# Indexer of the sparse attention: rectify on ScalarE, weight and sum the heads on the matrix unit

## The reference, cut to what matters

```python
def block(xs):                       # one block of 128 queries; two blocks in all
    qb, qib, wb, pb, start = xs
    dots = jnp.einsum('bqhd,bsd->bqhs', qib, k_idx)            # 16 index heads of 64
    I = jnp.einsum('bqh,bqhs->bqs', wb, jax.nn.relu(dots))     # weight and sum the heads
    I = jnp.where(causal[None], I, -jnp.inf)
    _, sel = lax.top_k(I, top_k)                               # 64 keys for each query
    ...                                                        # attention over these keys
```

## Time and profile before

| | us |
|---|---|
| median of three timed runs | 2379.22 |
| lowest and highest of them | 2372.86, 2379.34 |
| the profiled execution | 2371.06 |
| its span | 2369.3 |
| PE, DVE busy | 2004.3 (85%), 1880.9 (79%) |
| ACT, POOL busy | 1173.7 (50%), 312.3 (13%) |

### The profile page before, as it was taken

One profiled execution on the slowest core, in us unless ns is written; L12 is line 12 of the kernel. 1 busy time (PEld: TensorE's weight loads), 2 busy tenths in 40 slices (PEclk: granted clock), 3 DMA queues, 4 the chain that ended last, 5 costly groups with the idle time before them and its releaser, 6 DMA issues. The chain is left out here.

```text
span 2369.3 us, 33971 instructions
## 1 busy us (share of the span) xinstructions
PE 2004.3 (85%) x13220; PEld 1835.7 (77%) x13220; DVE 1880.9 (79%) x2572; ACT 1173.7 (50%) x1609; POOL 312.3 (13%) x214
## 2 busy tenths in 40 slices
PE   5998897898887888889877768699878979987898
PEld 4887797898876878877777756599768868877786
DVE  6877867858876988888889876668988765898886
ACT  5555444335445644444444445544455574445554
POOL 0001321320110013210001000031121100321110
PEclk9998998999999989899988889789999988998999
DMA  6774454559987656679877776566777757575786
GB/s 210 258 231 128 150 178 144 186 175 322 307 297 258 206 188 208 194 240 331 306 245 246 256 248 232 185 197 196 233 230 259 262 163 240 165 255 192 255 265 223
DMA packets 295341, 536.89 MB, mean 227 GB/s; under 512 B 31880, under 2 KB 40973, under 8 KB 294157
## 3 DMA queue, kind: packets, MB, share of 16 engines
q1 hardware_dynamic: 294893, 532.62, 69.4%
q10 hardware_dynamic: 288, 2.10, 0.2%
HBM read 532.55 MB, written 2.10 MB: 226 GB/s over the span
## 5 line engine op out<-in xcount | busy, mean ns | idle before, releaser
L1630 DVE SCALAR_TENSOR_TENSOR ring_r<-ring,w 128x1024 fp32r<-128x1024 f32 x807 | 999.0, 1256 | 389.7 <-ACT w L1235 384.5
L143 PE MATMUL ps<-hh_r,w 128*128 128x256 f32 x4160 | 1106.0, 303 | 150.1 <-DVE ring_r L1630 134.4
L1235 ACT ACTIVATE w<-ring 128x1024 fp32r<-128x1024 f32 x807 | 833.6, 1053 | 756.9 <-DMA ring<-in_w_in 324.1
L143 PE MATMUL ps<-hlo,ring_r 128*128 128x256 f32 x4160 | 1078.2, 296 | 0.0
L143 PEld LDWEIGHTS ps<-hh_r,w 128*128 128x128 f32 x4160 | 857.3, 206 | 178.5 <-DVE ring_r L1630 155.3
L143 PEld LDWEIGHTS ps<-hlo,ring_r 128*128 128x128 f32 x4160 | 856.7, 206 | 1.5 <-issue 1.2
L143 PE MATMUL ps<-w,AR_r 128*128 128x512 f32 x736 | 302.9, 412 | 31.0 <-DVE ring_r L1630 30.9
L1630 DVE SCALAR_TENSOR_TENSOR macc<-ring,sm,macc 128x512 f32<-128x512 f32 x360 | 304.3, 845 | 8.1 <-DMA ring<-in_w_mod 1.2
L143 PE MATMUL ps<-ring_r,AR_r 128*128 128x512 f32 x736 | 295.8, 402 | 0.0
L143 PEld LDWEIGHTS ps<-w,AR_r 128*128 128x128 f32 x736 | 143.0, 194 | 78.3 <-DVE ring_r L1630 48.9
L143 PE MATMUL ps<-AR 128*128 128x64 f32 (+5 forms) x1312 | 179.0, 298 | 17.8 <-DVE AR L1626 14.4
(11 more groups left out here) (176 smaller groups left out, 1556.7 us busy)
## 6 DMA issues: line engine op xcount, KB each, us to landing
ring<-in_w_in SPq DMA_DIRECT2D x408, 512.0 KB, 4.6
ring<-in_w_mod SPq DMA_DIRECT2D x192, 512.0 KB, 6.1
ring<-in_w_up SPq DMA_DIRECT2D x176, 512.0 KB, 4.7
ring<-in_w_out SPq DMA_DIRECT2D x96, 512.0 KB, 5.7
ring<-in_w_down SPq DMA_DIRECT2D x88, 512.0 KB, 5.8
ring<-in_w_branch_b SPq DMA_DIRECT2D x16, 512.0 KB, 5.5
ring<-in_w_branch_a SPq DMA_DIRECT2D x16, 512.0 KB, 5.8
X<-in_x SPq DMA_DIRECT2D x2, 1024.0 KB, 5.6
```

The source lines that it names most:

```text
L143: return e.matmul(o, l, x, start=start, stop=stop, skip_group_check=True)
L1235: return e.activation(o, i, ACT.Copy, scale=scale)
L1630: return e.scalar_tensor_tensor(o, a, s, b, op0, op1)
```

## The change

ACT rectifies the scores out of PSUM (two instructions for each head) into `IX0` and `IX1`, and makes four 128 x 128 diagonals `IWD` for each segment, the identity scaled by the two heads' weights for the two query blocks. PE multiplies diagonal and rectified scores and sums all heads in one PSUM bank (g, held from segment 0 to segment 8), always one segment behind the scores. DVE adds the masks straight from that bank in segment 8. POOL and DVE have no more work in segments 0 to 7.

```diff
@@ -183,9 +183,8 @@
     "upv": ["+s", "+z -s@up_dve.conv", "", "-z@up_dve.lo"],
     "bias": ["", *[s for i in range(12) for s in ("", "", f"+b -b@bias_act.e{i}")]],
     "scalex": [],
-    "indexer": ["+a +b -a@idx_dve.a0 -b@idx_dve.b0",
-                *[f"+a +b +s +z -s@idx_pool.g0{i} -z@idx_pool.g1{i} -a@idx_dve.a{i} -b@idx_dve.b{i}"
-                  for i in range(1, 8)]],
+    "indexer": ["+g +a +b -a@idx_act.x0 -b@idx_act.x0", *[f"+a +b -a@idx_act.x{i} -b@idx_act.x{i}" for i in range(1, 8)],
+                "-g@idx_dve.m1"],
     "kn": ["+s", "+z", "+b", "-b@kn_act.root", "-s@kn_dve.ka -z@kn_dve.ka"],
     "qn": ["+s", "", "+b", "-b@qn_act.root", "-s@qn_dve.inv"],
     "sparse": ["+a +b -a@sp_dve.l01 -b@sp_dve.l11", "", "", "", "+c +d -c@sp_act.pt0 -d@sp_act.pt1",
@@ -305,6 +304,7 @@
     Y2w = {n: [[carve(at, 512, dt=F32R) for at in c] for c in v] for n, v in (("a", YA2), ("b", YB2))}
     YAF, YBF = QA, QI
     W2 = 11008
+    IX0, IX1, IWD = carve(W2, 2, 128), carve(W2 + 256, 2, 256), carve(W2 + 768, 4, 128)
     IW = carve(W2 + 768, 2, S)
     MN0, MN1 = sel[:, 0:128], sel[:, 128:384]
     DM = carve(18432, 8, 256)
...
@@ -1125,6 +1125,15 @@
 
         def indexer(J, seg):
             L, = J.at
+            acc = pb(J, "g")
+            if 1 <= seg <= 8:
+                e.wait_ge(*idx_act.after(f"x{seg - 1}", L))
+                if seg == 1:
+                    hold(e, J, "g")
+                for hf in range(2):
+                    fp(acc[:, 0:128], IWD[:, 2 * hf, :], IX0[:, hf, :], seg == 1 and hf == 0, seg == 8 and hf == 1)
+                    q = fp(acc[:, 128:384], IWD[:, 2 * hf + 1, :], IX1[:, hf, :], False, seg == 8 and hf == 1)
+                q.then_inc(*idx_pe.step(f"s{seg - 1}", L))
             if seg < 8:
                 hold(e, J, "a", "b")
                 e.wait_ge(*qi_act.after("copy1", L, seg // 4))
@@ -1540,6 +1549,21 @@
             copy(VBB[:, 0, 512 * blk:512 * blk + 512], J.ps[0][:, :])
             copy(VBB[:, 1, 512 * blk:512 * blk + 512], J.ps[1][:, :]).then_inc(*vb_act.step("copy1", L, blk))
 
+        def indexer(J, seg):
+            L, = J.at
+            if seg < 8:
+                e.wait_ge(*wi_act.after("copy1", L))
+                if seg > 0:
+                    e.wait_ge(*idx_pe.after(f"s{seg - 1}", L))
+                for hf in range(2):
+                    for i in range(2):
+                        copy(IWD[:, 2 * hf + i, :], ident, scale=wi[:, i, 2 * seg + hf:2 * seg + hf + 1])
+                e.wait_ge(*idx_pe.after(f"p{seg}", L))
+                for hf, bk in ((0, pb(J, "a")), (1, pb(J, "b"))):
+                    fn(IX0[:, hf, :], bk[:, 0:128], ACT.Relu)
+                    q = fn(IX1[:, hf, :], bk[:, 128:384], ACT.Relu)
+                q.then_inc(*idx_act.step(f"x{seg}", L))
+
         def kn(J, seg):
             if seg == 0:
                 hold(e, J, "s")
@@ -1609,7 +1633,7 @@
                  "xpose": x_transposed, "norm": norm, "rope": rope, "mv": mv, "moba": moba, "bd": bd_evac, "convq": conv,
         for what, *a in steps:
             if what == "split":
@@ -2069,33 +2093,17 @@
 
         def indexer(J, seg):
             L, = J.at
-            a0, a1 = carve(W2, 2, 128), carve(W2 + 256, 2, 256)
-            if seg < 8:
-                e.wait_ge(*idx_pe.after(f"p{seg}", L))
-                if seg == 0:
-                    x0, x1 = a0, a1
-                    e.wait_ge(*wi_act.after("copy1", L))
-                else:
-                    hold(e, J, "s", "z")
-                    x0, x1 = pair(st(J, "s")[:, 0:256]), pair(st(J, "z"))
-                for hf, bk in ((0, pb(J, "a")), (1, pb(J, "b"))):
-                    hd = 2 * seg + hf
-                    ts(x0[:, hf, :], bk[:, 0:128], 0.0, MAX, wi[:, 0, hd:hd + 1], MUL)
-                    ts(x1[:, hf, :], bk[:, 128:384], 0.0, MAX, wi[:, 1, hd:hd + 1], MUL).then_inc(*idx_dve.step(f"{'ab'[hf]}{seg}", L))
             r0, r1 = IW[:, 0, 0:128], IW[:, 1, :]
             if seg == 8:
-                e.wait_ge(*idx_pool.after("g17", L))
-                tt(r0, a0[:, 0, :], a0[:, 1, :], ADD).then_inc(*idx_dve.step("h0", L))
-                tt(r1, a1[:, 0, :], a1[:, 1, :], ADD).then_inc(*idx_dve.step("h1", L))
-                e.wait_ge(*idx_dve.after("h0", L))
-                tt(r0, r0, causal0, ADD).then_inc(*idx_dve.step("r0", L, 0))
-                e.wait_ge(*idx_dve.after("h1", L))
-                tt(r1, r1, causal, ADD).then_inc(*idx_dve.step("r1", L, 0))
+                acc = pb(J, "g")
+                e.wait_ge(*idx_pe.after("s7", L))
+                tt(r0, acc[:, 0:128], causal0, ADD).then_inc(*idx_dve.step("m0", L))
+                tt(r1, acc[:, 128:384], causal, ADD).then_inc(*idx_dve.step("m1", L))
             if 8 <= seg <= 11:
                 for it in (2 * seg - 16, 2 * seg - 15):
-                    e.wait_ge(*idx_dve.after("r0", L, it))
+                    e.wait_ge(*(idx_dve.after("r0", L, it) if it else idx_dve.after("m0", L)))
                     e.max(mxa, r0).then_inc(*idx_dve.step("x0", L, it))
-                    e.wait_ge(*idx_dve.after("r1", L, it))
+                    e.wait_ge(*(idx_dve.after("r1", L, it) if it else idx_dve.after("m1", L)))
                     e.max(mxb, r1).then_inc(*idx_dve.step("x1", L, it))
                     e.wait_ge(*idx_dve.after("x0", L, it))
                     e.match_replace(r0, mxa, r0, -3e38).then_inc(*idx_dve.step("r0", L, it + 1))
@@ -2296,16 +2304,6 @@
                 tt(REL, mid(PQR[:, 128 * qt:128 * qt + 128], 8),
                    rep(PKC[:, 32 * kb + 8 * jh:32 * kb + 8 * jh + 8], 128), ADD).then_inc(*bias_pool.step(f"rel{i}"))
 
-        def indexer(J, seg):
-            L, = J.at
-            if 1 <= seg <= 7:
-                a0, a1 = carve(W2, 2, 128), carve(W2 + 256, 2, 256)
-                e.wait_ge(*idx_dve.after(f"b{seg}", L))
-                if seg > 1:
-                    e.wait_ge(*idx_pool.after(f"g1{seg - 1}", L))
-                tt(a0, a0, pair(st(J, "s")[:, 0:256]), ADD).then_inc(*idx_pool.step(f"g0{seg}", L))
-                tt(a1, a1, pair(st(J, "z")), ADD).then_inc(*idx_pool.step(f"g1{seg}", L))
-
         def kn(J, seg):
             if seg == 1:
                 s_, z = st(J, "s")[:, 0:256], st(J, "z")[:, 0:256]
@@ -2350,7 +2348,7 @@
                    MUL).then_inc(*glu_pool.step("y", *J.at))
 
         for what, *a in steps:
             if what == "phase" and a[0].kind in parts:
                 parts[a[0].kind](*a)
```

More of the change, by code:

```diff
@@ L365, in program @@
     ki_act, wi_act, qi_act, va_act, vb_act = (signal(f"{n}_act") for n in ("ki", "wi", "qi", "va", "vb"))
-    idx_pe, idx_dve, idx_pool = (signal(f"idx_{n}") for n in ("pe", "dve", "pool"))
+    idx_pe, idx_act, idx_dve = (signal(f"idx_{n}") for n in ("pe", "act", "dve"))
     kn_pe, kn_act, kn_dve, kn_pool = (signal(f"kn_{n}") for n in ("pe", "act", "dve", "pool"))
@@ L1611, in scalar_program @@
                  "convk": conv, "convv": conv, "z": z_evac, "gdn": gdn, "gb": gb, "merge": merge, "upg": up, "upv": up,
-                 "bias": bias, "ki": ki, "wi": wi_evac, "qi": qi, "va": va, "vb": vb, "kn": kn, "qn": qn,
+                 "bias": bias, "ki": ki, "wi": wi_evac, "qi": qi, "va": va, "vb": vb, "indexer": indexer, "kn": kn, "qn": qn,
                  "sparse": sparse, "rot": rot, "retain": retain, "glu": glu}
@@ L2352, in pool_program @@
         parts = {"moba": moba, "convq": conv, "convk": conv, "gdn": gdn, "merge": merge, "upv": up,
-                 "bias": bias, "indexer": indexer, "kn": kn, "sparse": sparse, "rot": rot, "retain": retain, "glu": glu}
+                 "bias": bias, "kn": kn, "sparse": sparse, "rot": rot, "retain": retain, "glu": glu}
         for what, *a in steps:
```

## The result

The changed kernel takes 2386.81 us (median of 13 runs, 2382.44 to 2392.34), the kernel before in the same session 2372.86 us (13 runs, 2366.11 to 2380.69). The ratio is 1.0057, with a 95% interval of 1.0043 to 1.0071: some 13.5 us slower. The forecast was 2388 us, made of +13.3 us on a base of 2371 to 2379.

What follows compares the result with a forecast made beforehand. PE was taken to bound the scoring and what follows the stage, DVE the search. Added matmuls and first-sum stands less saved waits gave +13.3 us: 2384.4 or 2392.5 by base, middle 2388 us, range 2376 to 2399.

Steps and rivals of the forecast that it cites:

- PE's matmuls: Segments 0 to 7: four fp32 diagonal matmuls a segment at 1.2 us, 9.6 us a layer, all added to PE.
- ACT's work: Each scoring segment: diagonals 1.25 us and rectifications about 0.95 us, 2.35 us with signals, without holding PE up.
- Rival C: Scoring steps: ACT becomes the bound through overheads or table loads, PE waiting up to 0.5 us a step; +7 us, chance 0.12.
- The stand at the first sum: Segment 0's sums: PE stands until ACT is done, 1.5 us in the first layer and 2.9 us in the second.
- The waits in the search: Segments 8 to 12: PE's waits for DVE, 4.5 and 5.8 us in the two layers, are saved whole.
- The margin: Search: DVE's splits come ahead of PE's need for them, with 0.9 us in hand at the tightest.
- B's first half: Behind the stage: one or both falls of the granted clock, about 3 us each, stay away; 2385 or 2382 us, chance 0.16.
- Its second half: Start of the stage: PE's new stand of 2.9 us brings a clock fall; +2 to +6 us, chance 0.13.
- The sum of the stage: Both layers' stages: matmuls plus stand less saved waits, +6.6 us and +6.7 us, together +13.3 us.
- D: DVE-bound stretches behind 1656 us: DVE's lead takes up the delay, leaving +3 to +6 us, 2380 us; chance 0.12.
- E: Search: its early start, without POOL's sums, outweighs PE's added work; -6 us, 2369 us, chance 0.05.
- A: Scoring segments: four sum matmuls cost only 0.36 us, so the time doesn't move, 2371 to 2379 us; chance 0.07.

Runs made afterwards that it cites:

- e1: Changed kernel with each segment's four diagonal matmuls issued twice: 2408.19 us, ratio 1.0156 to the kernel before.
- e2: Changed kernel with one four-column matmul in place of the four diagonal matmuls in segments 1 to 7: 2369.25 us, ratio 0.9989 to the kernel before.
- e3: Changed kernel with diagonals and rectified scores written as fp32r instead of fp32: 2372.81 us, ratio 1.0002 to the kernel before.
- e4: Changed kernel with segment 0's diagonals made earlier, right after the head weights are copied: 2383.63 us, ratio 1.0053 to the kernel before.
- e8: Changed kernel with both fp32r sums and segment 0's diagonals made early: 2371.34 us, ratio 1.0008 to the kernel before.
- e5: Kernel before, but ACT rectifies and DVE weights and sums, without POOL or PE for the sums: 2365.49 us, ratio 0.9982.
- e6: Kernel before with two chunks instead of one between the search segments 8 to 12, nothing else changed: 2364.55 us, ratio 0.9972.
- e7: Kernel before with ACT rectifying, DVE weighting and summing, and two chunks between the search segments: 2363.50 us, ratio 0.9968.

## Why the prediction was right

*What bounds.* PE in the scoring part, DVE in the search, PE behind the stage. Confirmed from both sides: doubled matmuls came out undiminished (e1), and taken away they gave all back (e2, e3). The mechanism was right; that the total came within 1.2 us of 2388 is partly luck, as the terms below were off by more than that and partly cancel, and the base was taken at 2374.7 where the 13 runs gave 2372.86.

*PE's matmuls*: 1.2 us a set was too low by 0.1. The regular ones cost 1.31 and the last 1.18, so 7 x 1.31 + 1.18 = 10.4 us a layer instead of 9.6. The nearest row, the attention's scores, was the right one; its 1.22 us was read at a group followed by a GEMM, as the last set is, whereas the others stand ahead of more fp32 work. The sum missed 1.6 us by it.

*ACT's work*: forecast 1.25 + 0.95 = 2.20 us (2.35 with signals); the rows show 1.28 + 0.96 less overlap, 2.15 us, and no stall in any regular step. Rival C fell. By the Trainium skill (page "ScalarE: Activation LUTs", section "Table sets: the hidden batching unit") relu sits in every table set: the trace agrees, since no table load lies between the rectifications and kn's and qn's roots. The Trainium skill, same page, section "Rules for kernel authors", gives relu to VectorE; here a rectification of 128x256 out of PSUM took ACT 378 ns, and DVE needed 472 with its weighting. The two aren't the same work, so the trace of this case neither bears the rule out for fp32 nor contradicts it; the prediction's "doesn't agree" says too much.

*The stand at the first sum*: forecast 1.5 and 2.9 us, measured 2.04 and 1.39. The mechanism holds (e4 took just the first diagonals out of it), but both sizes were off, one low and one high: they hang on where ACT happens to be with its two splits, and that differs between executions (the same place had 1.30 and 2.04 in e3, 1.66 and 2.32 in e2). The sums of 4.4 and 3.4 us hid it, which is luck.

*The waits in the search* vanished whole, as worked out, with 16.40 of 16.40 us busy. The margin, forecast at 0.9 us, was 0.4 in the first layer: the fourth split ends at 1624.77, and PE begins its chunk at 1625.17 (DVE's and PE's timelines after).

```profile
1623.55 1.22 DVE L1654 SCALAR_TENSOR_TENSOR ring_r<-ring,w 128x1024 fp32r<-128x1024 f32 x1
```

```profile
1625.17 0.28 PE L143 MATMUL ps<-hh_r,w 128*128 128x256 f32 x1
```

The margin counted: with sums 0.84 us shorter a set (e3), DVE is later at the masks, and the search is 0.34 us late once a layer.

*The clock.* Both falls behind the value block came again (0.62 in 1634 to 1643 and in 2078.4 to 2087.3), so B's first half fell. Its price of 3 us a fall was about right (3.4), though by a wrong reading: the first 1.1 us of the earlier trace rows still ran at the full clock, at 0.11 us a matmul, so that these 32 matmuls alone lost about 2.2 us and the rest lies behind them. Its second half came true in one layer: the fall behind the stand of 2.04 us cost 3.54 - 2.27 = 1.3 us, and a little in the chunk behind it.

*The sum of the stage.* From the first scores to the last chunk of the search, layer 0 grew from 44.65 us to 53.6 (+9.0) and layer 1 from 46.10 to 51.5 (+5.4): +14.4 instead of +13.3, for +0.8 in each for the matmuls, +0.5 and -1.5 for the stands, about +1.6 in the first for the clock; -0.5 us in each is left over and stays unexplained. The ratio gives 13.5 us, between the forecast and the stages' sum.

The two profiled spans differ by 17.2 us, since the first scores start 1.5 us later, the way between the stages is 5.4 us longer and the way behind the second 4.0 shorter. None of this can be put down to the change by single executions. Ahead of the first scores, where the kernels do the same work but for a few copies on ACT in e4 and e8, the ten profiled executions needed 1565.3 to 1578.0 us. From qn's sums in the first layer to the scores of the second, they needed 399.5 to 408.4 us, after taking out the search's waits, with before at 399.5 and e5 at 408.4. The two kernels that keep POOL's sums are the lowest there (before 399.5, e6 400.5), and with e2 the highest behind the second stage (317.2, 316.6 and 318.4 us against 310.7 to 315.6 for the rest). In the sum of both ways they are still second and third lowest of the ten, 700.4 and 701.1 us in a range of 699.8 to 705.9; single executions can't show whether that comes from POOL's sums. What makes that scatter, beside the two lengths of the clock's fall, stays open. D, E and A fell as well: e1's added time came out whole, the matmuls weren't cheap, and no gain for DVE and POOL beyond the search's waits shows in the times.

## What to carry to other kernels

Before moving work between engines, look which engine is the bound in that very stage: 61 us of relief for DVE and POOL were worth the 10.3 us of PE's waits and no more that shows, and the 21 us of new PE work counted in full. Where one engine has a short late phase (a search, a reduction at the end), spread its steps over more of the bound engine's work before rewriting it: here one line of spacing won about 7 us (interval 2 to 11) where the rewrite lost 13.5. If sums must go to the matrix unit, price them from rows of the same format and depth with the same neighbours, since the format alone made a factor of 2.8 here.

## What the runs showed of the hardware

- Four matmuls of 128 rows and 768 columns in all cost 1.31 us on fp32 operands and 0.47 us on fp32r operands; the indexer's scores, four fp32 matmuls of 64 rows in the same columns, 1.01 us. One matmul of four columns, with its 128x128 weights, still added 0.14 us to a step.
- A stand of PE isn't always followed by a fall of the granted clock. It fell behind stands of 2.04 us (after, layer 0), 2.04 us (e3, layer 1, 0.70 in the 2.1 us behind it) and 2.82 us (e1, layer 1), and stayed at 1.00 behind 1.66 and 2.32 us (e2), 1.40 (e1, layer 0), 1.39 (after, layer 1) and 0.87 (e4). What tells the cases apart beside the length isn't settled. From the table of stretches of e1, behind the first sum of layer 1:

```profile
2040.00:2042.00 2.00, 2.00 (x9) 1.72 (x8) 0.88 (x1) 0.00 (x0) 1.31 (x1) 0.50 0.00 0
```

  And of e2, at the same place:

```profile
2005.00:2007.00 2.00, 2.00 (x17) 1.65 (x18) 1.10 (x1) 2.00 (x6) 0.72 (x1) 1.00 0.38 144
```
- DVE's split took 1.69 us in the stage before, while POOL's additions ran, and 1.23 us in the same place after, with POOL silent. In e5 and e7, where DVE kept the weighting and only POOL's sums went, it took 1.22 us there too. So it goes with POOL's sums and not with DVE's own load; which of POOL's accesses slows it isn't shown.
